# Norm factors spread by transposes instead of matmuls, and a fifth PSUM bank with another order of the weights' halves in the delta rule projection

## The reference, cut to what matters

```python
def rmsnorm(x, g):
    xf = x.astype(jnp.float32)
    y = xf * lax.rsqrt(jnp.mean(xf * xf, axis=-1, keepdims=True) + EPS)
    return (y * g.astype(jnp.float32)).astype(x.dtype)

def gated_deltanet_mixer(h, w_in, conv_w, a_log, dt_bias, out_norm, w_out):
    proj = h @ w_in
    qkv = causal_depthwise_conv_silu(proj[..., :o1], conv_w)
    z = proj[..., o1:o2].reshape(b_sz, t_len, GDN_HEADS, GDN_DV)
    b_logit = proj[..., o2:o2 + GDN_HEADS]
    a_in = proj[..., o2 + GDN_HEADS:]
    ...
```

## Time and profile before

| | us |
|---|---|
| median of 3 runs | 2246.17 |
| the runs | 2246.27, 2246.17, 2242.71 |
| profiled execution | 2243.35 |
| its span, first to last instruction | 2241.4 |
| TensorE busy in it | 2161.1 |
| VectorE, ScalarE, GpSimd busy | 1147.9, 817.7, 38.6 |

### The profile page before, as it was taken

The page is one execution under the profiler, slowest core; times in us unless marked ns, Lnnn a source line. Parts: engine busy times, 40 slices in busy tenths (PEclk is TensorE's granted clock), DMA queues, the critical chain, the costliest instruction groups (busy, mean ns, idle before and its releaser), DMA issues. The chain is left out here.

```text
span 2241.4 us, 26186 instructions
## 1 busy us (share of the span) xinstructions
PE 2161.1 (96%) x10762; PEld 1711.7 (76%) x10762; DVE 1147.9 (51%) x1703; ACT 817.7 (36%) x1169; POOL 38.6 (2%) x34
## 2 busy tenths in 40 slices
PE   8999999999999998999989999998999899999998
PEld 6776678888888876777877888887786577888886
DVE  5574765442542578787836444323723726444323
ACT  4324753331232464442524222213415724232212
POOL 0120000000000000000100000000000000000000
PEclk9999999999999999998999999999999999999999
DMA  4220012222222222233122222222241022222221
GB/s 171 83 87 26 1 57 104 94 94 94 94 94 94 94 81 71 108 117 90 39 76 75 94 94 94 94 94 79 94 169 37 2 94 75 94 94 94 94 94 66
DMA packets 43110, 190.67 MB, mean 85 GB/s; under 512 B 15520, under 2 KB 16224, under 8 KB 22384
## 3 DMA queue, kind: packets, MB, share of 16 engines
q1 hardware_dynamic: 40656, 184.78, 24.5%
q10 hardware_dynamic: 2336, 4.23, 0.5%
HBM read 185.25 MB, written 3.74 MB: 84 GB/s over the span
## 5 line engine op out<-in xcount | busy, mean ns | idle before, releaser
L236 DVE TENSOR_TENSOR weights_low<-weights_raw,weights_high 128x2048 fp32r<-128x2048 f32 (+1 forms) x164 | 372.5, 2271 | 580.4 <-ACT weights_high L209 580.3
L426 PE MATMUL psum<-split,weights_high 128*128 128x512 f32 (+1 forms) x1496 | 593.4, 397 | 13.7 <-DVE weights_low L236 6.0
L428 PE MATMUL psum<-split,weights_low 128*128 128x512 f32 (+1 forms) x1496 | 596.4, 399 | 0.0
L427 PE MATMUL psum<-split,weights_high 128*128 128x512 f32 (+1 forms) x1496 | 591.2, 395 | 0.0
L209 ACT CAST weights_high<-weights_raw 128x2048 fp32r<-128x2048 f32 (+1 forms) x164 | 309.7, 1888 | 569.5 <-PE psum L428 538.0
L426 PEld LDWEIGHTS psum<-split,weights_high 128*128 128x128 f32 (+1 forms) x1496 | 281.6, 188 | 84.4 <-issue 10.7
L427 PEld LDWEIGHTS psum<-split,weights_high 128*128 128x128 f32 (+1 forms) x1496 | 281.7, 188 | 70.3
L428 PEld LDWEIGHTS psum<-split,weights_low 128*128 128x128 f32 (+1 forms) x1496 | 281.5, 188 | 66.8
L428 PE MATMUL psum<-hidden_high,weights_low 128*128 128x512 f32 x256 | 102.1, 399 | 0.0
L427 PE MATMUL psum<-hidden_low,weights_high 128*128 128x512 f32 x256 | 100.9, 394 | 0.0
L426 PE MATMUL psum<-hidden_high,weights_high 128*128 128x512 f32 x256 | 100.4, 392 | 0.0
(11 more groups left out here) (472 smaller groups left out, 3026.6 us busy)
## 6 DMA issues: line engine op xcount, KB each, us to landing
weights_raw<-in_weights SPq DMA_DIRECT2D x161, 1024.0 KB, 4.9
minus_c<-minus_c_rows ACTq DMA_DIRECT2D x16, 256.0 KB, 7.7
x_stream<-in_x SPq DMA_DIRECT2D x4, 512.0 KB, 6.8
gdn_in_grown<-gdn_rows SPq DMA_DIRECT2D x4, 512.0 KB, 4.7
chain_grown<-gdn_rows SPq DMA_DIRECT2D x4, 512.0 KB, 3.8
out<-end_results SPq DMA_DIRECT2D x8, 256.0 KB, 2.0
table<-rope_tables SPq DMA_DIRECT2D x1, 1024.0 KB, 11.9
weights_raw<-in_weights SPq DMA_DIRECT2D x1, 768.0 KB, 4.2
```

Source lines behind the costliest of these rows:

```text
L236: self.nc.vector.tensor_tensor(out=self.low[:, n % 2, 0:width], in0=self.raw[:, n % 2, 0:width], in1=self.high[:, n % 2, 0:width].bitcast( ...
L426: nc.tensor.matmul(bank, wh, ah, start=first, stop=False)
L427: nc.tensor.matmul(bank, wh, al, start=False, stop=False)
L428: return nc.tensor.matmul(bank, wl, ah, start=False, stop=last)
```

## The change

In all five functions that spread factors, `nc.tensor.matmul(bank, column repeated, identity)` becomes `nc.tensor.transpose(bank, column repeated, identity)`. In the projection tile 4 goes to bank 5, and the later tiles go round banks 0 to 3 one place later (tile 5 to bank 0, tile 8 to bank 3); tile o above 4 waits until o-4 tiles have freed their banks, where it waited for o-3 from tile 4 on; the gate banks follow. ScalarE makes the high half of chunk start+5 after the tap of tile 5, where it made it after that of tile 3. VectorE makes the low half of chunk start+4 after tile 1, where it made it after tile 3. The other halves keep their places.

```diff
@@ latent_spreads, spread_factor, spread_factors, spread_residual, Closing.tensor (one of five alike)
-                    last = nc.tensor.matmul(psum[:, self.spread_bank, j * P:(j + 1) * P],
-                                            self.stat[:, 2, j:j + 1].broadcast_to([P, P]), identity, start=True, stop=True)
+                    last = nc.tensor.transpose(psum[:, self.spread_bank, j * P:(j + 1) * P],
+                                            self.stat[:, 2, j:j + 1].broadcast_to([P, P]), identity)
@@ gdn_project
-            gate_banks = ((0, 1, 2, 3), (4, 6, 7, 5))
+            def bank_of(o):
+                return o if o < 4 else 5 if o == 4 else (o - 1) % 4
+
+            gate_banks = ((3, 0, 1, 2), (4, 6, 7, 5))
@@ TensorE
-                            pe.wait_ge(bank_free, o - 3)
-                            whole_tile(chunk_of(o), o % 2, o % 4, split)
+                            if o > 4:
+                                pe.wait_ge(bank_free, o - 4)
+                            whole_tile(chunk_of(o), o % 2, bank_of(o), split)
@@ ScalarE
-                            nc.scalar.activation(mixed[:, o % 2, :], psum[:, o % 4, :], ACT.Copy,
+                            nc.scalar.activation(mixed[:, o % 2, :], psum[:, bank_of(o), :], ACT.Copy,
                                                  scale=conv[:, tile + 3 * n_tiles:tile + 3 * n_tiles + 1]).then_inc(tap_done, 1)
-                            if o in (1, 3):
+                            if o == 1:
                                 weights.split_high(act, Chunk(chunk_of(o + 2) + 2))
-                            if o % 2 and o >= 7:
+                            if o % 2 and o >= 5:
                                 weights.split_high(act, Chunk(chunk_of(o) + 2))
@@ VectorE
-                                    out=mixed[:, o % 2, back:T], in0=psum[:, o % 4, 0:T - back], scalar=conv[:, at:at + 1],
+                                    out=mixed[:, o % 2, back:T], in0=psum[:, bank_of(o), 0:T - back], scalar=conv[:, at:at + 1],
...
-                            c = chunk_of(o) + 2
-                            if o % 2 and o >= 2:
-                                weights.split_low_vector(dve, c)
+                            if o == 1:
+                                weights.split_low_vector(dve, chunk_of(o + 2) + 2)
+                            if o % 2 and o >= 5:
+                                weights.split_low_vector(dve, chunk_of(o) + 2)
```

More of the change, by code:

```diff
@@ L542, in latent_spreads @@
                                     at = TT * tile + j
-                                    last = nc.tensor.matmul(psum[:, 4 + tile, j * P:(j + 1) * P],
-                                                            latent_stat[:, 2, at:at + 1].broadcast_to([P, P]), identity, start=True, stop=True)
+                                    last = nc.tensor.transpose(psum[:, 4 + tile, j * P:(j + 1) * P],
+                                                            latent_stat[:, 2, at:at + 1].broadcast_to([P, P]), identity)
                                 last.then_inc(latent_spread, 1)
@@ L1639, in spread_factors @@
                 for j in range(TT):
-                    last = nc.tensor.matmul(psum[:, self.factor_bank, j * P:(j + 1) * P],
-                                            self.stat[:, 7, j:j + 1].broadcast_to([P, P]), identity, start=True, stop=True)
+                    last = nc.tensor.transpose(psum[:, self.factor_bank, j * P:(j + 1) * P],
+                                            self.stat[:, 7, j:j + 1].broadcast_to([P, P]), identity)
                 last.then_inc(self.spread, 1)
@@ L1645, in spread_residual @@
                 for j in range(TT):
-                    last = nc.tensor.matmul(psum[:, self.residual_bank, j * P:(j + 1) * P],
-                                            self.stat[:, 6, j:j + 1].broadcast_to([P, P]), identity, start=True, stop=True)
+                    last = nc.tensor.transpose(psum[:, self.residual_bank, j * P:(j + 1) * P],
+                                            self.stat[:, 6, j:j + 1].broadcast_to([P, P]), identity)
                 last.then_inc(self.residual_spread, 1)
@@ L1709, in tensor @@
                 for j in range(TT):
-                    last = nc.tensor.matmul(psum[:, bank, j * P:(j + 1) * P], self.stat[:, 2, j:j + 1].broadcast_to([P, P]),
-                                            identity, start=True, stop=True)
+                    last = nc.tensor.transpose(psum[:, bank, j * P:(j + 1) * P], self.stat[:, 2, j:j + 1].broadcast_to([P, P]),
+                                            identity)
                 last.then_inc(self.spread, 1)
```

## The result

The changed kernel takes 2232.26 us in the median of 4 runs (2230.8 to 2232.72), the kernel before 2244.44 (2241.26 to 2246.27). The profiled execution took 2232.38 us, its span is 2230.6, 10.8 less than that of before.

What follows compares the result with a forecast made beforehand. TensorE, busy for 96% of the span, was taken as the bound. Projection 5.2 plus spreads 5.6 gave 10.8 us off the 2246.17 median: 2235.4, rounded to 2235, with an 8-in-10 range of 2229.5 to 2241.5.

Steps and rivals of the forecast that it cites:

- both parts: Part one, the start of the delta rule projection, gains 5.2 us; part two, the thirteen spreads as transposes, gains 5.6 us.
- Tiles 4 to 7 without a gap, and a new gap before tile 8: Projection: TensorE's gaps before tiles 4 and 6 go; it waits 6.0 us before tile 8 for VectorE's low half.
- the 0.9 of the final norm's groups: Two spreads at the projection's start save 0.9 us that only lengthens the gap before tile 8; counted at nothing.
- VectorE's chain by pitches: Projection: old-trace pitches from tile 1's last step at 856.95 put the low half for tiles 8 and 9 at 878.3.
- The tail: Projection: slow matmuls at low clock behind the new gap before tile 8 cost 2.0 us, between 1.3 and 2.7.
- Carried to the end of the stage: Projection: the gain of 5.2 us at tiles 8 and 9 follows through the rest of the stage to its end.
- Dense spreads: Eight groups of four on the path, amid dense matmuls, gain 0.43 us each as transposes, 3.4 us together.
- Closings: Three spread groups with TensorE idle ahead and VectorE waiting gain 0.75, 0.50 and 0.95 us, together 2.2.
- Rival 1: The projection gains only 1.5 us, its gap before tile 8 or low clock lasting longer: 2239 us; chance 0.12.
- Rival 2: In the spreads, transposes cost what the matmuls did, through mode switching or the broadcast: 2241 us; chance 0.08.
- Rival 3: Transposes don't count as work for the clock, so low stretches follow dense spreads: slower, 2260 us; chance 0.03.
- Rival 4: More gain: 0.7 us from a short tail and 3.6 from shorter low clock behind the closings: 2231 us; chance 0.07.

Runs made afterwards that it cites:

- e2: The kernel before with only the projection edits (new banks, new order of the halves), spreads still matmuls: ratio 0.9973 to the kernel before.
- e7: The changed kernel with 24 extra matmuls, results unused, issued in the gap before tile 8: ratio 0.9931 to the kernel before.
- e8: The changed kernel with each of the thirteen groups of four transposes issued twice: ratio 0.9974 to the kernel before.
- e3: The kernel before with only the fifth bank, the halves in the old order and spreads still matmuls: ratio 0.9986 to the kernel before.
- e4: The kernel before with only the new order of the halves, four banks and spreads still matmuls: ratio 0.9968 to the kernel before.
- e1: The kernel before with only the thirteen spreads as transposes, projection as it was: ratio 0.9965 to the kernel before.
- e5: The changed kernel with four banks again, keeping transposes and the new order of the halves: ratio 0.9936 to the kernel before.
- e6: The changed kernel (five banks) with both weight halves of tiles 8 to 11 made one tile earlier: ratio 0.9924 to the kernel before.
- e9: The changed kernel with four banks and the halves for tiles 8 to 11 after tiles 4 and 6: ratio 0.9928 to the kernel before.

## Why the prediction was right

The forecast was 2235, 10.8 us below the median then shown; measured are 2232.26 and 11.9 by the ratio. Faster was given 0.92, and it is faster. The profiled execution took 2232.38 us where 2232.5 was worked out; the 2.7 us between 2235 and the median come from the base, since the 2.8 us by which the median of before lay above its profiled execution have no like in the changed kernel. The mechanisms came as forecast, in both parts. That the two spans differ by the very 10.8 us of the sum is luck: 1.02 us stood there ahead of every edit, 1.8 were lost where nothing was changed, and three of the terms below miss by about half a microsecond, one way or the other.

- **Tiles 4 to 7 without a gap, and a new gap before tile 8.** Right in place, releaser and length: 6.0 us plus the 0.9 of the final norm's groups was forecast, 6.73 stands in the trace, and 6.03 where those groups are matmuls (e2).
- **VectorE's chain by pitches.** From tile 1's last step (856.95, now 853.55, 3.40 earlier) to the low half of tiles 8 and 9 the working gave 878.3 - 856.95 = 21.35 us; the trace has 874.84 - 853.55 = 21.29.
- **The tail.** 2.0 was taken, 2.55 came: tiles 8 and 9 lie between 874.90 and about 888.75, 13.8 us instead of 11.3. That is why the projection gave 4.70 and not 5.2. e7 removes the tail alone and wins 2.42.
- **Carried to the end of the stage.** The shift is 8.06 at tile 9 (896.92 to 888.86) and 8.10 at 1015.05: nothing of it was lost in between, as forecast. At the start of the delta rule chain 0.5 less was left; from the last low half to there the twelve profiles take 14.88 to 16.52 us, so that is chance.
- **Dense spreads.** 0.43 a group forecast, 0.44 measured (0.80 to 0.36), and 0.44 again by doubling (e8). In these traces four transposes cost 0.36 to 0.44, half the matmuls' time. The Trainium skill ("TensorE: Matmul & The Clock Gate", Terms) says that the transpose mode is four times faster for FP32; by that a group would have come to 0.20, an estimate that the traces don't bear out. A transpose is one record at the pitch at which an f32 matmul has two.
- **Closings.** 0.75, 0.50 and 0.95 forecast, 1.08, 0.05 and 1.43 measured; the sum, 2.56 for 2.2, is near, the parts are not. What I had put down to the instructions is largely the clock: the first and third groups ran at the low clock before and take 0.65 us now, the second ran at the full clock before (1.16 us for eight records) and at the low one now, 1.11 us for four. The other profiles show which of this was chance. With matmuls the three groups take 1.16 to 1.18, 2.07 to 2.08 and 2.07 to 2.08 us in e2, e3 and e4 alike, so the profile of before was unusually slow at the first (1.73) and unusually fast at the second (1.16). With transposes they take 0.65, 1.11 to 1.12 and 0.65 in the changed kernel and in e1, e5, e6 and e7; only e9 has the low clock at the first, 1.11. At the third closing every profile with matmuls has the low clock and every one with transposes the full one, also e8 with its eight (1.09); why is not shown. The windows of the second and third in the changed kernel (before, the granted clock was 1.00 in the one and 0.50 in the other), the granted clock third from the end:

```profile
1549.30:1550.60 1.30, 1.11 (x4) 0.71 (x4) 0.11 (x1) 0.00 (x0) 0.00 (x0) 0.52 0.00 0
1837.60:1839.00 1.40, 0.65 (x4) 0.41 (x4) 0.66 (x2) 0.00 (x0) 0.00 (x0) 1.00 0.00 0
```

- **Rivals.** Rival 1 (the projection pays 1.5) falls: the gap is 6.73 us and the stretch 4.70 shorter. Rival 2 (transposes no cheaper) falls with e1, and the matmuls' 0.80 against the transposes' 0.36 decides it. Rival 3 (transposes drop the clock) falls too: the matmul behind the group at 29.31 is 0.48 us long, as behind the matmul group of the earlier trace rows, and in the 5 us from the start of each of the ten dense groups of the changed kernel the granted clock is 1.00. Rival 4 (a short tail, and 3.6 us more behind the closings) falls as well: the tail was longer than taken, and behind the three closings the shift grows by 0.45, 1.01 and 0.47 us, of which one dense spread each explains 0.44. Part 4 of the same page of the Trainium skill says that the full clock doesn't engage for transposes; here groups of four or eight amid dense matmuls let nothing fall.

What I did not see: that in the profiles the fifth bank is worse than nothing beside this order. The working had all that was needed, since it showed VectorE's low half at 878.3 whether TensorE waits before tile 4 or before tile 8. With four banks TensorE ends tile 7 at 878.4, in time, and the gap before tile 4 with its slow matmuls costs nothing more. With five the same wait stands at the end, with its slow matmuls behind it.

## What to carry to other kernels

When TensorE waits for a chain on another engine, an extra buffer that lets it run ahead only moves the idle time to where the chain ends. The slow matmuls behind the gap then stand on the path, where earlier they fell into the wait (e5 and e7 against the changed kernel). Beside the old order the bank did pay (e3, 4.63 us of the stretch), for there the chain itself waited for TensorE's products of tile 5. Shorten the chain, or take the wanted step forward in it, first (e4 against e3, e6 against the changed kernel). Write down the chain with the pitches of the old trace: here it hit a time seven steps on within 0.1 us. To repeat a column over a tile, an f32 transpose against the identity costs half of an f32 matmul here (0.36 against 0.80 us for four).

## What the runs showed of the hardware

- In the start of the projection slow matmuls (0.43 us from start to start) followed every gap of 2.7 to 7.0 us, and their number had no fixed relation to it: 8 after 2.71 (e6, from the sixth matmul on), 13 after 3.44 (before) and 14 after the same in e4, 13 after 4.35 in e5 and 8 after the same in e9, 8 after 4.34 in e1, 6 after 5.50 before and 11 after the same in e1, 9 after 6.03 in e2 and 7 after the same in e8, 12 after 6.73 and 6.71 (changed, twice), 7 after 7.04 (e3). After the 1.27 us of e7, with its extra matmuls ahead, there were none. One such matmul costs 0.19 us, so this decides about 1 us a time, and makes profiles differ.
- Such chance stands elsewhere too. At the start of the kernel, ahead of every edit, the first square sum began between 22.61 (e1) and 24.19 us (e4). Behind the delta rule chain the changed kernel's profile had the low clock once more, 0.83 in this window where the same work had 1.00 before (1123.00 to 1133.00 there), and most of 1.3 us of the gain are gone there:

```profile
1115.30:1125.30 10.00, 9.79 (x37) 7.79 (x38) 3.73 (x4) 2.49 (x3) 0.00 (x0) 0.83 0.31 106
```

- Such differences, a few of 1 to 2 us each, are of the size by which the runs of one kernel differ (2241.26 to 2246.27). That they are the cause was not tried. The stretch within the stage repeats to 0.01 us in two profiles of the changed kernel (168.85 both times, with twelve slow matmuls each), and differences of 2 us were read there. But it has the tail in it, which chance moves by about 1 us (e5 and e9): the bank's 1.65 and 2.38 us are what these profiles show, and with a tail of seven, as in e8 (1.51 us instead of the changed kernel's 2.47), the 2.38 would be about 1.4, an estimate.
